# Transposes ahead of scores and masks in TensorE's order of a sparse attention stage

## What is computed

```python
def dsa_attention(q, k, v, ix_q, ix_k, ix_w, positions, rel_bias):
    ...
        _, sel = lax.top_k(score, topk)
        valid = sel <= q_idx[None, :, None]
        ...
        logits = jnp.einsum('bqhd,bqkd->bqhk', qb, kg) * (dh ** -0.5)
        ...
        logits = logits + jnp.moveaxis(bias, -1, 2)
        p = jax.nn.softmax(jnp.where(valid[:, :, None, :], logits, -jnp.inf), axis=-1)
        return jnp.einsum('bqhk,bqkd->bqhd', p, vg)
```

## Time and profile before

| what | value |
|---|---|
| median of 3 runs | 1379.31 us (1378.16 to 1379.43) |
| the profiled execution's own time | 1379.81 us |
| its span, first to last instruction | 1378.1 us |
| mean granted clock of TensorE | 0.981 |
| TensorE busy (matmul) | 1287.8 us, 93% |
| VectorE, ScalarE, POOL busy | 775.8, 608.3, 181.3 us |

### The profile page before, as it was taken

The page is one execution under the profiler, slowest core; times in us unless marked ns, Lnnn a source line. Parts: engine busy times, 40 slices in busy tenths (PEclk is TensorE's granted clock), DMA queues, the critical chain, the costliest instruction groups (busy, mean ns, idle before and its releaser), DMA issues.

```text
span 1378.1 us, 17854 instructions
## 1 busy us (share of the span) xinstructions
PE 1287.8 (93%) x6530; PEld 971.6 (71%) x6538; DVE 775.8 (56%) x1582; ACT 608.3 (44%) x1130; POOL 181.3 (13%) x302
## 2 busy tenths in 40 slices
PE   3589999999889999999999999999988999999998
PEld 2277767656558888888888776665555888888887
DVE  7956577778653333354436667777855323435442
ACT  3335456666564223223324455666656322323330
POOL 3400111123330000000000021112333000000000
PEclk9899999999989999999999999999999999999999
DMA  6432221110241322222332311110024133232321
GB/s 167 115 115 84 70 62 32 46 31 1 81 135 31 122 92 92 92 92 92 101 83 92 93 62 62 33 54 22 17 74 126 50 104 92 92 95 90 121 93 61
DMA packets 118424, 109.15 MB, mean 79 GB/s; under 512 B 34496, under 2 KB 101056, under 8 KB 118336
## 3 DMA queue, kind: packets, MB, share of 16 engines
q1 hardware_dynamic: 110096, 107.96, 26.1%
q10 hardware_dynamic: 8240, 0.03, 0.3%
HBM read 100.64 MB, written 7.34 MB: 78 GB/s over the span
## 4 chain that ended last, share of the span: by engine, by line
PE 74%; DVE 10%; ACT 7%; issue 5%; POOL 2%; SPq 1%; DMA 0%; DVEq 0%; ACTq 0%
PE bank L736 19%; PE bank L738 19%; PE bank L737 19%; PE bank L844 2%; PE bank L1037 2%; PE bank L1010 2%; PE bank L1053 2%; DVE probs L1874 1%; POOL reach L466 1%; PE bank L868 1%; DVE w_lo L637 1%; ACT soft L1333 1%; PE bank L1066 1%; ACT soft L1335 1%; PE bank L885 1%
## 5 line engine op out<-in xcount | busy, mean ns | idle before, releaser
L736 PE MATMUL bank<-h_hi,w_hi 128*128 128x512 f32 (+1 forms) x928 | 360.1, 388 | 3.6 <-DVE h_lo L1567 2.2
L738 PE MATMUL bank<-h_hi,w_lo 128*128 128x512 f32 (+1 forms) x928 | 352.7, 380 | 0.0
L737 PE MATMUL bank<-h_lo,w_hi 128*128 128x512 f32 (+1 forms) x928 | 352.6, 380 | 0.0
L637 DVE TENSOR_TENSOR w_lo<-raw,w_hi 128x2048 fp32r<-128x2048 f32 (+2 forms) x98 | 187.7, 1916 | 129.0 <-ACT w_hi L631 128.9
L631 ACT CAST w_hi<-raw 128x2048 fp32r<-128x2048 f32 (+2 forms) x100 | 159.3, 1595 | 118.7 <-PE bank L738 118.7
L736 PEld LDWEIGHTS bank<-h_hi,w_hi 128*128 128x128 f32 x928 | 175.7, 189 | 46.9 <-issue 9.4
L738 PEld LDWEIGHTS bank<-h_hi,w_lo 128*128 128x128 f32 x928 | 175.7, 189 | 33.5
L737 PEld LDWEIGHTS bank<-h_lo,w_hi 128*128 128x128 f32 x928 | 175.7, 189 | 32.5 <-issue 1.9
L1508 ACT ACTIVATE gate<-bank,gains 128x512 f32<-128x512 f32 x48 | 33.0, 688 | 166.1 <-PE bank L738 166.1
L2019 POOL TENSOR_SCALAR probs<-probs,stat 128x128 f32<-128x128 f32 (+3 forms) x128 | 75.4, 590 | 167.7 <-DVE stat L1829 162.1
L1037 PE MATMUL bank<-mats,probs 128*128 128x128 f32 x320 | 57.7, 298 | 18.3 <-ACT probs_dsa L1481 18.3
(11 more groups left out here) (221 smaller groups left out, 2184.9 us busy)
## 6 DMA issues: line engine op xcount, KB each, us to landing
raw<-in_w_in SPq DMA_DIRECT2D x56, 1024.0 KB, 5.2
raw<-in_w_branch SPq DMA_DIRECT2D x12, 1024.0 KB, 5.1
raw<-in_w_out SPq DMA_DIRECT2D x8, 1024.0 KB, 5.1
bias<-bias_dram SPq DMA_DIRECT2D x16, 256.0 KB, 3.0
bias<-bias_dram SPq DMA_DIRECT2D x16, 192.0 KB, 2.6
x_sb<-in_x SPq DMA_DIRECT2D x4, 512.0 KB, 5.1
bias_dram<-bias_out SPq DMA_DIRECT2D x8, 256.0 KB, 2.9
raw<-in_w_in SPq DMA_DIRECT2D x4, 512.0 KB, 4.6
```

Of the source, the lines that this page charges most:

```text
L637: e.tensor_tensor(w_lo[:, s % RING, a:b], raw[:, s % RAW, a:b], w_hi[:, s % RING, a:b].bitcast(F32), ALU.subtract).then_inc(*lo_signal(nam ...
L736: pe.matmul(out_ap, lh, rh, start=start and i == 0, stop=False)
L737: pe.matmul(out_ap, lh, rl, start=False, stop=False)
L738: mm = pe.matmul(out_ap, ll, rh, start=False, stop=stop and i == n - 1)
```

## The change

In steps j = 4 to 15 (`DSA_AV` + 1 up to `DSA_STEPS` - 1) TensorE issues the transposes of step j-2 first, then scores and masks of step j, then the values of step j-3. In steps 0 to 3 and 16 to 18 its order is as before. All instructions, their waits and signals, and the queues of all other engines are the same.

```diff
                 for j in range(DSA_STEPS + DSA_AV):
+                    early = DSA_AV + 1 <= j < DSA_STEPS
+                    if early:
+                        for u, o, h, t in dsa_units(j - DSA_T):
+                            t_of(u)
                     if j < DSA_STEPS:
                         for u, o, h, t in dsa_units(j):
                             s_of(u)
...
-                    if 0 <= j - DSA_T < DSA_STEPS:
+                    if 0 <= j - DSA_T < DSA_STEPS and not early:
                         for u, o, h, t in dsa_units(j - DSA_T):
                             t_of(u)
                     if 0 <= j - DSA_AV < DSA_STEPS:
```

## The result

The changed kernel takes **1414.39 us** (median of 4 runs, 1411.80 to 1414.71), the kernel before in the same comparison 1379.37 us. The ratio is 1.0254, 95% interval 1.0242 to 1.0267: slower by 35 us, as forecast (1415.6 us). The profiled execution took 1414.28 us.

A forecast was written before the change was run, and what follows sets the result against it. A ring from bias sum through exponentials, ScalarE's copies and transposes to the next bias sum was taken as the bound; scores and first mask would join it. At mixed clock, 1379.8 + 35.8 = 1415.6 us, range 1397 to 1431.

The forecast's parts named there:

- the two stretches: Bias sum of sparse step 3 to that of step 15, in layers 0 and 1: 43.06 and 43.70 us before.
- round: Four sparse steps, one per key width (128, 256, 384, 512); three per layer in the changed steps.
- the chain: Changed steps: bias sum, exponentials, two copies, both units' transposes, both units' scores, first mask, next bias sum; only values outside.
- Sum at full clock: Changed steps, TensorE never slowed: 17.9 us per round, 53.7 us for three, +20.6 us over both layers.
- Sum at 1.2 GHz: Changed steps, TensorE always at the lower clock: 22.55 us per round, 67.7 for three, +48.6 us over both layers.
- The share of the lower clock: Changed steps: 60% of the time at 1.2 GHz, granted clock 0.70, chosen between two ends; gives +35.8 us.
- Clock kept up: Rival: TensorE's clock would not fall in the changed steps; +20.6 us, 1400.4 us, chance 0.12.
- Clock down throughout: Rival: TensorE at the lower clock in all changed steps, four idle gaps a round; +48.6 us, 1428.4 us, chance 0.08.
- Hidden anyway: Rival: same wait for the copies, TensorE's idle time only moved in the sparse stage; 1380 us, chance 0.07.
- faster: Rival: earlier transposes release ScalarE's copies, removing its 8.0 us of waits for transposes; 1371.8 us, chance 0.03.
- ring: Before, sparse stage: bias sum, exponentials, copies of pair j-2, transposes of pair j-1, next bias sum; scores and masks outside.

The follow-up runs named there:

- the kernel with fillers: Six matmuls with unread results added after the values of each of steps 4 to 15, against the changed kernel; 1406.12 us, ratio 1.0202 to the kernel before.

## Why the prediction was right

- **Where the loss is.** Said: in the two stretches alone, 86.8 us before. It is: 34.1 of the 34.4 us by which the span grew.
- **What waits.** Said: the bias sum waits for a mask and not for a transpose; TensorE idles before every transpose. Both are in the source views, 56.8 us and 39.8 us. The idle times themselves were put at 1.9 to 2.9 us and are 0.9 to 2.5 in the round shown. The prediction allowed at most 0.5 us for the values in front of them; they take 0.44 to 1.09 us at full clock and, in this round, up to 1.55 at the lower. This had no price, since the values are beside the chain, but it made the gaps look longer than they are.
- **Sum at full clock**, 17.9 us a round: 17.7 measured, in the kernel with fillers. Widths one by one are within 0.1 us.
- **Sum at 1.2 GHz**: steps of 128 and 256 within 0.1 us, with the division named above the table; no whole round at 1.2 GHz was seen.
- **The share of the lower clock.** Chosen as 60% of the time, granted 0.70. It was about 48%, 0.77 and 0.75. This was the weakest term, said to be a choice, and the stretches came out at 59.7 and 61.2 us against 61.3 each. The steps at the lower clock were those of width 128 and 256, and on these two fall 2.6 of the some 4.7 us that a round wholly at the lower clock would add, so that less of the time bought nearly the same loss. In sum 35.0 us by the medians, against 35.8. The mechanism was read from the rows; that the total came within 1 us, with a share that was off by 12 points, is luck.
- **The split** of the 35.8 us was 20.6 for the order with the clock whole and 15.2 for the clock. Measured: 6 x 17.7 = 106.2, less 86.8, is 19.4; and 14.6.
- **Rivals.** Clock kept up (1400.4): the clock fell, at idle times of at most 2.9 us before the transposes (2.7 in layer 0). The Trainium skill, page "TensorE: Matmul & The Clock Gate", section "Why this matters for your kernels", ties the fall to longer gaps than these; the traces of both kernels disagree with it. In the kernel before, transposes after an idle time of 2.04 us (at 373.92) ran at 1.2 GHz, six in 1.51 us. Clock down throughout (1428.4): it rose again in each round. Hidden anyway (1380) and faster (1371.8): refuted by the stretches; ScalarE's waits for a transpose are still 8.2 us in 4 cases, and both before and after all four lie behind the last changed step, the longest at 438.77 and 1106.16 in the changed kernel.

What the prediction did not see is that 7.4 us of the kernel before were themselves lost to the clock, in a gap that the profile put down to ScalarE's copy: it took 0.84 as given.

## What to carry to other kernels

When instructions are moved ahead on an in-order queue, look at what the moved ones wait for: all that they pass inherits the wait. Here transposes whose bank was still to be copied were put ahead of scores that had been free, and 4.5 us a round went onto the chain. The same move was cheap when the copy had first been put ahead of the exponentials on the other engine. The copies alone, moved ahead in all steps without touching TensorE, were worth 1.5%. Open such a ring at the place where a result waits behind younger work, and check with one run whether the clock of TensorE follows the idle time.

## What was not expected of the hardware

Matmuls that compute nothing made the kernel faster: 48 of them in the gaps of the order before raised the granted clock in the stretches from 0.84 to 1.00 and took 0.5% off (1371.23 against 1378.29 us). In the changed kernel the low clock settled into step with the rounds: in five of the six rounds the matmuls of the steps of width 128 and 256 ran at 1.2 GHz and the scores of those of 384 and 512 at 2.4 GHz, with idle gaps of only 0.9 to 2.9 us between them. Nor does the length of one gap decide: in the kernel before, six transposes took 0.85 us (full clock) right after 2.60 us of idle time at 1038.53, and the scores behind them, at 1040.34, took the 1.23 us of 1.2 GHz. The fall came when TensorE was already at work again.
